# Gathering an expert pair's tokens with the selection as the stationary operand

## The reference

```python
cap = 2 * n // N_EXPERTS                       # 64 tokens for each of 16 experts
aff = softmax(x @ w_router)
gate, idx = lax.top_k(swapaxes(aff, 1, 2), cap)
xin = x[idx]                                   # (16, 64, 1024)
hid = silu(xin @ w_e1[e]) * (xin @ w_e3[e])    # (16, 64, 2816)
y = (hid @ w_e2[e]) * gate
out = segment_sum(y, idx)                      # back to 512 rows
h = layer_norm(alpha * h + out)
```

## Time and profile before

| | us |
|---|---|
| median of three runs | 2100.98 |
| the profiled execution | 2098.37 |
| its span, first to last instruction | 2096.4 |
| TensorE busy | 1944.9 (93%) |
| VectorE busy | 652.0 (31%) |
| ScalarE busy | 389.9 (19%) |
| GpSimd busy | 252.1 (12%) |
| mean granted clock of TensorE | 0.97 |

### The profile page before, as it was taken

How to read it: one execution, slowest core, us unless ns; L and a number is a source line. 1 busy time by engine, 2 the same in 40 slices (tenths; PEclk the granted TensorE clock), 3 DMA queues, 4 the chain that set the end, 5 groups by cost and what they waited for, 6 DMA issues and landing times.

```text
span 2096.4 us, 20184 instructions
## 1 busy us (share of the span) xinstructions
PE 1944.9 (93%) x8502; PEld 991.6 (47%) x8502; DVE 652.0 (31%) x1149; ACT 389.9 (19%) x707; POOL 252.1 (12%) x268
## 2 busy tenths in 40 slices
PE   8999999999999997999889889889889889979978
PEld 4656554466678755353353343343334335325322
DVE  6599757588865352001001001001001001001003
ACT  1444313289810021000000000000000000000001
POOL 1787400065300000000000000000000000000001
PEclk9899999999999998999999999999999999999999
DMA  5631304133332576999999999999999999999994
GB/s 146 135 97 56 115 15 149 48 133 121 121 141 95 218 307 252 394 430 428 436 427 429 429 434 409 431 432 427 436 426 428 429 432 416 436 428 430 434 426 200
DMA packets 77945, 638.16 MB, mean 304 GB/s; under 512 B 19820, under 2 KB 33568, under 8 KB 60704
## 3 DMA queue, kind: packets, MB, share of 16 engines
q1 hardware_dynamic: 65216, 628.98, 73.3%
q10 hardware_dynamic: 12640, 7.89, 1.3%
HBM read 626.98 MB, written 9.88 MB: 304 GB/s over the span
## 4 chain that ended last, share of the span: by engine, by line
PE 67%; DMA 21%; DVE 2%; ACT 2%; issue 0%; DVEq 0%
PE ps L1074 66%; DMA arena<-in_w_e 21%; ACT arena L725 1%; PE ps L1546 1%; ACT L725 0%; PE ps L1185 0%; DVE arena L2190 0%; PE ps L1248 0%; PE ps L1302 0%; DVE arena L2184 0%; DVE arena L2090 0%; DVE arena L2092 0%; PE ps L1439 0%; PE ps L1410 0%; DVE arena L1885 0%
## 5 line engine op out<-in xcount | busy, mean ns | idle before, releaser
L1074 PE MATMUL ps<-arena 128*64 128x512 f32 (+8 forms) x7968 | 1881.3, 516 | 115.9 <-DMA arena<-in_w_e 101.2
L1074 PEld LDWEIGHTS ps<-arena 128*64 128x64 f32 (+2 forms) x7968 | 930.5, 170 | 1046.5 <-issue 864.4
L725 ACT ACTIVATE arena<-ps 128x512 f32<-128x512 f32 (+6 forms) x304 | 165.4, 574 | 1588.8 <-PE ps L1074 1076.8
L2155 DVE TENSOR_TENSOR arena<-arena,ps 128x512 f32<-128x512 f32 (+1 forms) x48 | 30.3, 645 | 839.1 <-PE ps L1074 839.1
L717 POOL TENSOR_TENSOR arena<-arena 128x1024 f32<-128x1024 f32 x3 | 7.1, 2353 | 1365.5 <-ACT arena L725 1365.5
L725 ACT ACTIVATE arena<-arena 128x128 f32<-128x128 f32 (+10 forms) x261 | 117.7, 509 | 71.6 <-DVE arena L2114 19.0
L2164 DVE TENSOR_TENSOR arena<-arena,ps 128x512 f32<-128x512 f32 x48 | 33.1, 690 | 282.7 <-PE ps L1074 282.7
L725 ACT ACT_TABLE_LOAD x74 | 94.9, 1283 | 24.1 <-issue 22.4
L1868 DVE SCALAR_TENSOR_TENSOR arena<-arena 128x512 f32<-128x512 f32 x80 | 63.5, 794 | 2.8
L677 POOL TENSOR_TENSOR arena<-arena 128x768 f32<-128x768 f32 x16 | 28.5, 1780 | 179.3 <-PE ps L1248 128.4
L1670 DVE TENSOR_TENSOR arena<-arena 128x320 f32<-128x320 f32 x48 | 29.5, 676 | 0.6
(11 more groups left out here) (206 smaller groups left out, 690.3 us busy)
## 6 DMA issues: line engine op xcount, KB each, us to landing
arena<-in_w_e SPq DMA_DIRECT2D x79, 5632.0 KB, 28.6
arena<-in_w_e SPq DMA_DIRECT2D x24, 1408.0 KB, 14.2
arena<-in_w_e SPq DMA_DIRECT2D x12, 2816.0 KB, 23.3
arena<-in_w_in SPq DMA_DIRECT2D x9, 2048.0 KB, 8.5
arena<-cumulative_scratch SPq DMA_DIRECT2D x16, 768.0 KB, 4.9
arena<-in_w_e SPq DMA_DIRECT2D x7, 1536.0 KB, 6.9
arena<-in_w_e SPq DMA_DIRECT2D x3, 3072.0 KB, 24.2
arena<-in_w_in SPq DMA_DIRECT2D x5, 1536.0 KB, 6.5
```

The costliest lines, as they stand in the source:

```text
L725: return act.activation(out, in_, func, **kw)
L1074: return pe.matmul(out, lhsT, rhs, start=a, stop=z)
L2155: tt(o, o, ps[:, 3 + i, 0:w], ALU.mult).then_inc(s.hid_ready, 1)
```

## The change

- The gather has `sel[:, c]` as the stationary operand and 512 columns of h as the moving one: four products for a half of the features, into one bank, as slots by features (`gathered(p, j, c)`). ScalarE copies the bank to a staging place (`token_rows`; the tile `hid`, or `ye` for the first pair). `tokens_turned` transposes its four blocks of 128 (stride 4) into another bank, and ScalarE copies these to `xin` (`token_columns`).
- First pair: half 0, the first product of half 1, the turn of half 0 and the second product of half 1 stand before `up(0, 0)`; the other two products and the turn of half 1 follow its rows k = 0, 1 and 2.
- Later pairs: half `which` is gathered after row k = 3 of `up(x, which)` of the odd expert, and both halves are turned between `down(x, 0)` and `down(x, 1)`.
- Expert 15: the sums of c = 0 and 1 stand after row k = 3 of `up(15, 1)`; three of c = 2 and 3 between the down halves; one behind them. The banks of the end are given by `final_bank`.
- The last expert's second half of w = 1 is cut into rows 0 to 2, 2 to 3 and 3 to 4, and both halves of its down weight into [0, 3, 6, 9, 11]. By `ring_places` the piece of rows 0 to 2 then lies in the rest of the ring behind the third unit, and waits for no row of experts 13 to 15; the pieces are 136 in place of 130.

```diff
@@ -144,7 +144,7 @@
         (1, 0): [0, 1, 2, 3, 4], (1, 1): [0, 2, 4], (1, 2): [0, 6, 11], (2, 0): [0, 2, 4], (2, 1): [0, 2, 4],
-        (EXPERTS - 1, 2): [0, 11] if j == 0 else [0, 6, 9, 11]}.get((x, w), [0, RUN[w]])
+        (EXPERTS - 1, 1): [0, 4] if j == 0 else [0, 2, 3, 4], (EXPERTS - 1, 2): [0, 3, 6, 9, 11]}.get((x, w), [0, RUN[w]])
     return [(x, w, j, r0, r1) for x in range(EXPERTS) for w in range(3) for j in range(2)
@@ -371,6 +371,10 @@
         ye = hT.rearrange("p a b -> p (a b)")
+        tok_rows = lambda p: hid if p else ye
+        tok_bank = lambda p, j: (7, 0)[j] if p else (7, 6)[j]
+        col_bank = lambda p, j: (1, 2)[j] if p else (3, 4)[j]
+        final_bank = ((0, 1), (2, 7), (3, 4), (5, 6))
@@ -1014,17 +1018,15 @@
-            def token_columns(p):
-                for j in range(2):
-                    act.wait_ge(s.xin_ps, KT + 2 * p + j - 1)
-                    f(xin[:, 4 * j:4 * j + 4, :].rearrange("p a b -> p (a b)"), ps[:, j, :], ACT.Copy).then_inc(s.xin_copied, 1)
-            def first_token_columns():
-                for k in range(KT):
-                    act.wait_ge(s.xin_ps, k + 1)
-                    f(xin[:, k, :], ps[:, 6 + k % 2, P * (k // 2):P * (k // 2) + P], ACT.Copy).then_inc(s.xin_copied, 1)
+            def token_rows(p, j):
+                act.wait_ge(s.xin_ps, 4 * p + (j + 1 if p else 2 * j + 1))
+                f(tok_rows(p)[:, 512 * j:512 * j + 512], ps[:, tok_bank(p, j), :], ACT.Copy).then_inc(s.xin_copied, 1)
+            def token_columns(p, j):
+                act.wait_ge(s.xin_ps, 4 * p + (j + 3 if p else 2 * j + 2))
+                f(xin[:, 4 * j:4 * j + 4, :].rearrange("p a b -> p (a b)"), ps[:, col_bank(p, j), :], ACT.Copy).then_inc(s.xin_copied, 1)
@@ -1045,7 +1047,9 @@
-            first_token_columns()
+            for j in range(2):
+                token_rows(0, j)
+                token_columns(0, j)
             for x in range(EXPERTS):
@@ -1054,7 +1058,10 @@
                 elif p + 1 < PAIRS:
-                    token_columns(p + 1)
+                    for j in range(2):
+                        token_rows(p + 1, j)
+                    for j in range(2):
+                        token_columns(p + 1, j)
                 expert_rows(x)
@@ -1501,22 +1508,25 @@
-            def gathered(o, kk):
-                cols = [h[:, c, 512 * (kk // 4):512 * (kk // 4) + 512].rearrange("q (p t) -> q t p", t=4)[:, kk % 4, :] for c in range(TT)]
+            def gathered(p, j, c):
+                return mm(ps[:, tok_bank(p, j), :], sel[:, c].rearrange("p a b -> p (a b)"), h[:, c, 512 * j:512 * j + 512], c == 0, c == TT - 1)
+            def gather(p, j):
+                pe.wait_ge(s.sel_built, p + 1)
+                if j:
+                    pe.wait_ge(s.silu_half, 3 * 2 * p)
                 for c in range(TT):
-                    r = mm(o, cols[c], sel[:, c].rearrange("p a b -> p (a b)"), c == 0, c == TT - 1)
-                return r
-            def first_gather(k):
-                gathered(ps[:, 6 + k % 2, P * (k // 2):P * (k // 2) + P], k).then_inc(s.xin_ps, 1)
-            def gather(p, j):
-                pe.wait_ge(s.sel_built, p + 1)
-                pe.wait_ge(s.silu_half, 3 * 2 * p)
-                for k in range(4):
-                    r = gathered(ps[:, j, P * k:P * k + P], 4 * j + k)
+                    r = gathered(p, j, c)
+                r.then_inc(s.xin_ps, 1)
+            def tokens_turned(p, j):
+                pe.wait_ge(s.xin_copied, 4 * p + (j + 1 if p else 2 * j + 1))
+                blocks = tok_rows(p)[:, 512 * j:512 * j + 512].rearrange("q (p t) -> q t p", t=4)
+                for t in range(4):
+                    r = pe.transpose(ps[:, col_bank(p, j), P * t:P * t + P], blocks[:, t, :], ident)
                 r.then_inc(s.xin_ps, 1)
@@ -1525,7 +1535,7 @@
                     if x == 0 and which == 0:
-                        pe.wait_ge(s.xin_copied, k + 1)
+                        pe.wait_ge(s.xin_copied, 2 + 2 * (k // 4))
                     for i, (c0, n_) in enumerate(BANKS):
@@ -1533,10 +1543,21 @@
                     row_used(r, x, which, k // 4, k % 4)
-                    if x == 0 and which == 0 and k + 2 < KT:
-                        first_gather(k + 2)
-                    if k == 3 and which == 0 and x and not e:
+                    if x == 0 and which == 0 and k < 2:
+                        r = gathered(0, 1, k + 2)
+                        if k:
+                            r.then_inc(s.xin_ps, 1)
+                    if x == 0 and which == 0 and k == 2:
+                        tokens_turned(0, 1)
+                    if k == 3 and x and not e and which == 0:
                         scatter(x // 2 - 1)
+                    if k == 3 and e and x + 1 < EXPERTS:
+                        gather(x // 2 + 1, which)
+                    if k == 3 and which and x + 1 == EXPERTS:
+                        pe.wait_ge(s.silu_half, 3 * EXPERTS)
+                        for c in range(2):
+                            for j in range(2):
+                                sum_so_far(c, j)
@@ -1578,20 +1599,21 @@
-            def sums_so_far(c):
-                for j in range(2):
-                    mm(ps[:, 2 * c + j, :], ident, acc[:, c, 512 * j:512 * j + 512], True, False)
+            def sum_so_far(c, j):
+                mm(ps[:, final_bank[c][j], :], ident, acc[:, c, 512 * j:512 * j + 512], True, False)
...
             pe.wait_ge(s.wo_read, 2 * TT)
-            first_gather(0)
-            first_gather(1)
+            gather(0, 0)
+            gathered(0, 1, 0)
+            tokens_turned(0, 0)
+            gathered(0, 1, 1)
             for x in range(EXPERTS):
...
                 if x and x % 2 == 0:
-                    pe.wait_ge(s.xin_copied, KT + 2 * p)
+                    pe.wait_ge(s.xin_copied, 4 * p + 4)
                 if x % 2:
@@ -1599,30 +1621,26 @@
                     gates_transposed(p)
-                elif p + 1 < PAIRS:
-                    gather(p + 1, 0)
-                elif x % 2:
-                    pe.wait_ge(s.silu_half, 3 * EXPERTS)
-                    sums_so_far(0)
                 turn(x)
-                if x % 2 and p + 1 < PAIRS:
-                    gather(p + 1, 1)
                 if x % 2 == 0 and x:
...
                 down(x, 0)
+                if x % 2 and p + 1 < PAIRS:
+                    for j in range(2):
+                        tokens_turned(p + 1, j)
                 if x == EXPERTS - 1:
                     pe.wait_ge(s.hidT_copied, 3 * EXPERTS)
-                    for c in range(1, TT - 1):
-                        sums_so_far(c)
+                    for c, j in ((2, 0), (2, 1), (3, 0)):
+                        sum_so_far(c, j)
                 down(x, 1)
...
                 if c == TT - 1:
-                    sums_so_far(c)
+                    sum_so_far(c, 1)
                 for j in range(2):
-                    mm(ps[:, 2 * c + j, :], selgT[:, c, :], ye[:, 512 * j:512 * j + 512], False, True).then_inc(s.sc_ps, 1)
+                    mm(ps[:, final_bank[c][j], :], selgT[:, c, :], ye[:, 512 * j:512 * j + 512], False, True).then_inc(s.sc_ps, 1)
@@ -2141,7 +2159,7 @@
                 if p >= 1:
-                    dve.wait_ge(s.xin_ps, KT + 2 * p - 2)
+                    dve.wait_ge(s.xin_ps, 4 * p - 2 if p > 1 else 3)
                     dve.wait_ge(s.selT_ps, p)
@@ -2181,13 +2199,13 @@
                     dve.wait_ge(s.sc_ps, 2 * TT * (PAIRS - 1) + 2 * c + j + 1)
-                    n.done(dve.bn_stats(stats[:, j, :], ps[:, 2 * c + j, :]))
+                    n.done(dve.bn_stats(stats[:, j, :], ps[:, final_bank[c][j], :]))
                 n.wait()
...
                     o = slice(512 * j, 512 * j + 512)
-                    stt(acc[:, c, o], ps[:, 2 * c + j, :], mv[:, c, 0:1], lnrow[:, 0, o], ALU.subtract, ALU.mult).then_inc(s.ln2_rows, 1)
+                    stt(acc[:, c, o], ps[:, final_bank[c][j], :], mv[:, c, 0:1], lnrow[:, 0, o], ALU.subtract, ALU.mult).then_inc(s.ln2_rows, 1)
                 dve.wait_ge(s.ln2_std, c + 1)
```

More of the change, by code:

```diff
@@ L1502, in row_used @@
                     ins.then_inc(s.piece_used, 1)
-            def gathered(o, kk):
-                cols = [h[:, c, 512 * (kk // 4):512 * (kk // 4) + 512].rearrange("q (p t) -> q t p", t=4)[:, kk % 4, :] for c in range(TT)]
-                for c in range(TT):
-                    r = mm(o, cols[c], sel[:, c].rearrange("p a b -> p (a b)"), c == 0, c == TT - 1)
-                return r
-            def first_gather(k):
-                gathered(ps[:, 6 + k % 2, P * (k // 2):P * (k // 2) + P], k).then_inc(s.xin_ps, 1)
+            def gathered(p, j, c):
+                return mm(ps[:, tok_bank(p, j), :], sel[:, c].rearrange("p a b -> p (a b)"), h[:, c, 512 * j:512 * j + 512], c == 0, c == TT - 1)
             def gather(p, j):
                 pe.wait_ge(s.sel_built, p + 1)
-                pe.wait_ge(s.silu_half, 3 * 2 * p)
-                for k in range(4):
```

(6 more changed lines are left out.)

## The result

The changed kernel took 2088.15 us in the median of four runs (2086.02 to 2088.65), the kernel before 2100.04 in the same comparison (four runs, 2097.85 to 2101.42). The ratio is 0.9942, with a 95% interval of 0.9925 to 0.9960: 12 us less. The forecast was 2091.0 (2086.0 to 2095.5), 10 us less, and faster at 0.92.

A forecast was written before the change was run, and what follows sets the result against it. Weight loads pace the long stretch, with TensorE setting the start and tail. Gains of 7.5 (start) and 2.5 (tail), nothing in the stretch, sum to 10.0 us: 2088.4 profiled, 2091.0 on the runs' scale, range 2086 to 2095.5.

The forecast's parts named there:

- Rival 3: Whole expert stage: TensorE was the bound after all, seven pairs at 8 us, 56 more, 2035; chance 1%.
- The start: Expert stage's start: TensorE's earlier release of the 873.8 issue shifts the whole paced stretch by 7.5 us.
- Rival 1: Start: something other than TensorE sets the 873.8 load, so only the tail gains 2.5 us, 2098.5; chance 5%.
- The long stretch: About 880 to 2010 us: TensorE saves some 8 us a pair, covered by loads, worth nothing in time.
- No unit reached that: the queue was never dry there: Long stretch: whole units took at least 16.0 us to land, against 15.8 estimated for an idle queue.
- part B: From landing of expert 1's 2816 KB load to landing of expert 15's third unit; forecast difference 0.
- rival 2: Tail: no half-clock stretch and the late load lands on time, up to 5 us sooner, 2086; chance 17%.
- The tail: Expert 15's end: sums in the wait, no half clock, fewer sums between down halves; gain 2.5 us, bounds 0 and 6.
- four sums (3.43) fill that wait: Tail, after expert 15's third unit: four sums, 3.43 us, fill TensorE's wait to 2039.71 for a whole unit.
- The finer cuts of the last down unit bring nothing by themselves: Tail: the last landing is over 7 us ahead of down's end at 2074.6, so these cuts gain nothing alone.
- part C: From the landing of expert 15's third unit to the end of the span; forecast difference -2.5 us.
- rival 4: Long stretch: longer waits bring half clock, 5.5 us lost a unit, slower, up to 2105; chance 2%.

The follow-up runs named there:

- gather_late: Changed kernel with eight more 512-column products, results not used, ahead of the first gather: 2096.05 us, ratio 0.9979 to the kernel before.
- before_more: Kernel before, with the second half gather of each later pair done twice: 2139.35 us, ratio 1.0184 to the kernel before.
- first_only: Changed kernel with the later pairs' gather, the cuts and the sums put back, so new gather for the first pair alone: 2094.59 us, ratio 0.9978 to before.
- tail_gone: Changed kernel with the last expert's cuts and the end sums put back, both gathers new: 2091.26 us, ratio 0.9958 to before.
- sums_back: Changed kernel with the end sums in their old places and banks, cuts and gathers as changed: 2085.11 us, ratio 0.9935 to before.
- cuts_back: Changed kernel with the last expert's units cut as before, gathers and sums as changed: 2088.51 us, ratio 0.9949 to before.
- later_only: Changed kernel with the first pair's gather, the cuts and the sums put back: 2094.46 us, ratio 0.9980 to before.
- rows_by_pe: Changed kernel with more cuts in expert 15, and the second norm's two rows loaded once and spread by TensorE: 2080.20 us, ratio 0.9902 to before.

## Why the prediction was right, and where it was not

**What bounds it: right.** The loads pace the middle: 173 busy in place of 185 changed no rate, and 48 us more work cost 1.5 us in the medians. Rival 3 (2035) is refuted.

**The start: right in mechanism and size.** 7.5 us were forecast for the issue of the 2816 KB load; the profile gives 7.1, its landing 8.0, and `gather_late` shows the path one for one. About 1 us of the 7.1 was luck with the clock: at the 5.4 us of half clock that the kernel before had, the new start issues that load after 64.5 us and not 63.5, a gain of 6.1. The first up row came after 7.6 us and not 8.4, because the clock was at half for 3.5 us of the first products and not 5.4. DMA share from 802 to 842 did not rise over 0.8 as I wrote: 0.70, since the stage began 3.6 us later. Counted from the first product over 35.3 us it went from 0.66 to 0.77. Rival 1 (tail only, 2098.5) is refuted.

**The old gather's cost.** The new form's products cost 0.86 us each, as the rows of the tail said; against the old 2.2 us between two rows the change gained at the start. The rule of the Trainium skill that the next weights are loaded while a product runs ("TensorE: Matmul & The Clock Gate", Step-by-step) would have made the change lose about 1 us a pair, an estimate, and the traces disagree. The rows were the better guide. Why the small products cost so much, by their stride of 4 or by a new stationary operand for every 128 columns, no run separates.

**The long stretch: the failed step.** "A saving of TensorE work between about 880 and 2010 us is therefore worth nothing by itself" and "No unit reached that: the queue was never dry there". I had the least time to landing, 16.0, and an estimated floor, 15.8, side by side, and read 0.2 us as a margin. `before_more` shows loads on an empty queue at 16.0 to 17.0, so there was none. It was the edge of a pattern that came once a pair. Before, the landing of an odd expert's last up unit at 1070.1 and the issue that its first down unit's release allows at 1105.9 were 35.8 us apart, with both old gathers between; after, 23.4. In `first_only` that distance is 35.8 to 38.5, and three of the six loads land late. The medians give the later gathers 3.3 to 4.7 us and the profiles' part B about 2, where I had nothing. I had even named the reason (the tightest release follows the two old gathers) and drawn no value from it. The range took it in only through rival 2.

**The tail: sign right, parts wrong.** 2.5 us were forecast; the two profiles show 3.2, all profiles some 2, and `tail_gone` against the changed kernel 3.1 in the medians. But "four sums (3.43) fill that wait" was wrong: with the half-unit cut off there is no wait to fill, and by the trace the sums' new place costs about 2 us beside the old (`sums_back`; 3.0 in the medians). The gain is the cuts': alone they take part C to 66.2 us, the sums alone leave it at 69.8. "The finer cuts of the last down unit bring nothing by themselves" is doubtful too, by the profile of `cuts_back`. The profile of before was also unlucky, and part of what I took for the sums' gain was this: the wait of 2.19 us ahead of the fourth unit held a landing 1.3 us late. The half clock of 2040.8 to 2044.3 is no such accident. It stands at the same place in `tail_gone`, whose fourth unit landed on time:

```profile
2032.90 13.29 PE L1081 MATMUL ps<-arena 128*64 128x512 f32 x52 [1.95 <-DMA arena<-in_w_e]
```

In `first_only` and `later_only` these products take 11.60 us, without it, and part C is 68.9 us in place of 70.0.

So 7.5+0+2.5 = 10.0 came near the 12 measured by a start that was right, a stretch put at nothing that was worth 2 to 4, and a tail whose sum was about right with wrong parts. The last is luck.

**The clock, rival 4.** Waits grew and the mean clock fell from 0.97 to 0.95 between 1400 and 1600 us, without a cost there: the half clock fell into time that the loads fill. Between the start of the stage and the end of the tail no half-clock stretch was longer than 6.8 us. The Trainium skill ("TensorE: Matmul & The Clock Gate", HAM oscillation) describes a kernel in which every stretch of work runs cold; the trace agrees only in part, as the mean of 0.95 shows. Half clock costs time where TensorE is on the path: at the start and in the tail.

## What to carry to other kernels

In a stage that a full load queue paces, don't ask how much work an engine does, but how long it is, at the worst point of each period, from a landing to the release that the next load waits for; compare the least time from issue to landing with that of an idle queue, and call anything within 2 us of it no cover at all (here 16.0 to 18.0 us was the edge and 23.5 was not). At that point every us of work is paid; away from it 48 us more cost nothing that could be told from noise. At the end of such a stage, cut the last units fine enough that the engine keeps up with the landings, and only then ask what else stands in its path.

## What was not expected of the hardware

- The products of 128 columns of h (stride 4) against 128 moving columns cost 2.2 us for four between two up rows, 0.28 us a record; 512 moving columns with the same 128 rows of depth cost 0.43 a record. A quarter of the columns takes two thirds of the time.
- Landings of whole units come 13.3 us apart with 1.5 us extra in one of about 19 (14.9 us; in some profiles shared between two landings), 242 to 269 us from one to the next, also where no load came near an idle queue (`tail_gone`, `gather_late`).
- The part of the kernel before this stage took 802.5 to 807.8 us, with the same instructions in all kernels but `rows_by_pe`.
- Of 48 us more work on TensorE in the stretch only 27 came out of its waits for loads: with fewer waits there were 39 us less at half clock (107 to 68, from 1000 to 2000 us).
